# First block's down GEMM two steps late, its last three by token halves, last up step with stationary weights; edges and orders of two sister stages

## The chip, the cores and the metric

The kernel runs on one core of one Trainium2 chip. The metric is the device time of one execution in microseconds (us), taken as the median of several executions. TensorE, VectorE, ScalarE, GpSimd and SyncE are called PE, DVE, ACT, POOL and SP, as in the profile.

## What is computed

Two transformer stacks, one behind the other, on 256 tokens of width 1024, each with two layers, in float32. The part of the reference that the change touches is the feed-forward half of every layer, and the passage from one layer to the next:

```python
# first stack, per layer l
gu = jnp.einsum('bsd,df->bsf', x, w_ffn_in[l])
hidden = jax.nn.silu(gu[..., :D_FF]) * gu[..., D_FF:]
ffn = jnp.einsum('bsf,fd->bsd', hidden, w_ffn_out[l])
x = layer_norm(DN_ALPHA * x + ffn, ln2_g[l], ln2_b[l])
# second stack, per layer i
h = rms_norm_2(x, ffn_norm_g[i]) @ w_up[i]
h = depthwise_conv(h, conv_w[i], conv_b[i])
gate, up = jnp.split(h, 2, axis=-1)
x = x + (jax.nn.silu(gate) * up) @ w_down[i]
```

D_FF is 2816. The attention parts ahead of it (neighbourhood, differential and latent attention in the first stack, grouped attention and spatial gating in the second) are the same computation before and after; one order inside the neighbourhood attention changes.

## The kernel before

**Pieces.** Every weight matrix comes from memory in pieces of at most 128 x 2048 (1 MB). SP loads piece i into one of three buffers `raw`, once DVE has finished with piece i-3. ACT rounds it to `whi` (the matmul's narrower float format; L1098) and DVE subtracts to get the rest, `wlo` (L1585). This is called splitting. There are four slots of `whi`/`wlo`: piece i can be split when PE has used piece i-4. Activations are split in the same way (`xTh`/`xTl`, `aTh`/`aTl`, `bTh`/`bTl`), and every product is the sum of three matmuls, high x high, high x low and low x high.

**Two ways to multiply.** In `gemm` and `half` (L384 to L388, L480 to L482) the activations are the stationary operand, a half of 128 tokens (`th` 0 or 1) at a time, and the weights stream past, 512 columns per matmul. In `by_features` (L409 to L412) the weights are stationary, and the activations of all 256 tokens stream past: one matmul of 512 columns takes high weights with `xTh` and `xTl` at once, one of 256 columns takes low weights with `xTh`. It ends in two PSUM areas that have to be added, ACT copying one out (`low_out`) and DVE adding (`features_out`). Its result has features on the partitions, as the next GEMM wants it; that of `gemm` has tokens there, and has to be transposed on PE.

**The feed-forward of the first stack.** It has NSTEP = 11 steps. Step c has an up GEMM (two pieces, 256 gate and 256 up features) and a down GEMM (one piece). `up(0)` and `up(1)` are by tokens, with a transpose `h_turn` behind; steps 2 to 9 are by features in two pairs of PSUM banks (0,1 and then 2,3); step 10 is by tokens again, in halves that are mixed with the halves of the last two down GEMMs and with two half turns of the hidden block (L813). The down GEMM of step c-1 follows the up GEMM of step c. The hidden blocks alternate in `aTh`/`aTl`.

**Its end, the edge to the next layer.** When token half 0 of the last down GEMM is summed, DVE adds it to x (`add_down`, L1963, one operation), takes the moments (`stats`, L1592 and L1595), POOL raises the variance to the power -0.5 (L289, L291), DVE applies the norm (`apply`, four operations, L1602 and L1604, each pair ending a half of x), PE transposes that half (`turn_x`, L437), ACT rounds it to `xTh` (L1105, or L1117 with gains) and DVE writes `xTl` (L1611, or L1623 with gains). Then the same with token half 1. The next layer's first GEMM needs the transposed x and the next four pieces, here called N0 to N3. Every engine works strictly in the order in which its program was written, so a split stands before or behind these steps by hand.

**The feed-forward of the second stack** is two steps late already: `up(0)` by tokens, then `up_features(c)` for 1 to 10, and `down(c-2)` behind each. `up(0)` ends in banks 0 and 1, from which ACT takes it with a scale (L1533); `by_features` for step 1 begins in bank 0 too. PE transposes step 0 (`conv_turn`, L1027) inside step 1.

**Neighbourhood attention.** For g = 0 to 4 PE computes scores of a pair of heads, transposes probabilities (`turn_probs`, L547) and mixes them with values (`mix_pair`, L557), with parts of other GEMMs between. ACT copies the transposed probabilities out (`probs_out`, L1217); `catch` is the place at which ACT or DVE empties PSUM and splits what may be split, up to `ahead` pieces past those that PE has used.

## Time and profile before

| | |
|---|---|
| median of 3 runs | 1482.4 us (1482.22 to 1482.57) |
| the profiled execution's own time | 1482.46 us |
| its span | 1481.1 us |
| PE, busy share | 98% |
| DVE / ACT / POOL, busy share | 70% / 55% / 4% |
| granted TensorE clock | 0.999 of full speed |
| DMA, mean rate over the span | 176 GB/s |

The span is the time between the first and the last instruction of the profiled execution; 1.4 us of its own time lie around it. A matmul's end is modelled, and a matmul is pipelined with its neighbours, so that the busy share of PE overstates it: two starts in a row lie closer together than one duration. Lines named L... are those of the kernel before.

### The profile page before, as it was taken

Reading aid. Unit: us, or ns where it says so; the run is one execution under the profiler, and the core shown is the slowest. Engines: PE = TensorE matmul, PEld = TensorE weight load, DVE = VectorE, ACT = ScalarE, POOL = GpSimd, SP = SyncE. Lnnn points to the kernel's source line nnn. Section 1 sums busy time; section 2 is a strip of 40 time slices with the busy share of each in tenths; the row PEclk is TensorE's granted clock in tenths of the full one; section 3 lists DMA queues with packets and bytes.
Section 4 is the critical chain, followed back from the end, with each engine's and each line's share of the span. In section 5 each row is a group of like instructions: output and inputs, shape, how many; then the busy total and the mean of one; then the engine's idle time right before and its main releaser. Section 6 shows DMA issues by size and latency. Waiting matters only on the chain.

```text
span 1481.1 us, 19352 instructions
## 1 busy us (share of the span) xinstructions
PE 1451.0 (98%) x7547; PEld 1209.0 (82%) x7547; DVE 1044.1 (70%) x1413; ACT 816.3 (55%) x1163; POOL 65.3 (4%) x100
## 2 busy tenths in 40 slices
PE   6999999999999999999999999899999999999998
PEld 5788887888887787887888888788888888888887
DVE  5656885865556656786775565877888868778886
ACT  3555654444453455654444544586665567766563
POOL 2000000000001000000010000210000012000000
PEclk9999999999999999999999999999999999999999
DMA  8543643566564635543666556336565635356651
GB/s 320 180 153 127 238 170 118 189 228 198 192 206 143 215 118 157 191 138 132 194 230 196 174 186 211 116 114 199 171 198 186 227 127 171 122 175 199 203 184 57
DMA packets 167323, 261.06 MB, mean 176 GB/s; under 512 B 8768, under 2 KB 106720, under 8 KB 166720
## 3 DMA queue, kind: packets, MB, share of 16 engines
q1 hardware_dynamic: 166048, 252.03, 51.8%
q0 software_dynamic: 896, 6.74, 1.2%
q8 instruction: 60, 0.98, 0.3%
q10 hardware_dynamic: 288, 1.05, 0.2%
q14 instruction: 31, 0.25, 0.0%
HBM read 258.74 MB, written 1.05 MB: 175 GB/s over the span
## 4 chain that ended last, share of the span: by engine, by line
PE 83%; DVE 9%; ACT 3%; issue 2%; POOL 1%; DMA 1%; SPq 0%; DVEq 0%; ACTq 0%
PE ps L409 16%; PE ps L480 10%; PE ps L482 10%; PE ps L481 10%; PE ps L410 9%; PE ps L384 7%; PE ps L388 7%; PE ps L386 7%; DVE wlo L1585 3%; PE ps L412 2%; ACT whi L1098 1%; PE ps L534 1%; PE ps L557 1%; DVE x L1604 1%; DVE x L1602 1%
## 5 line engine op out<-in xcount | busy, mean ns | idle before, releaser
L1585 DVE TENSOR_TENSOR wlo<-raw,whi 128x2048 fp32r<-128x2048 f32 (+1 forms) x238 | 528.1, 2229 | 230.3 <-ACT whi L1098 230.3
L1098 ACT ACTIVATE whi<-raw 128x2048 fp32r<-128x2048 f32 (+1 forms) x238 | 441.8, 1866 | 145.0 <-PE ps L482 54.3
L409 PE MATMUL ps<-xT,whi 128*128 128x512 f32 x1008 | 356.4, 395 | 1.6 <-ACT proj L1533 1.6
L410 PE MATMUL ps<-xT,wlo 128*128 128x256 f32 x1152 | 311.1, 280 | 0.0
L480 PE MATMUL ps<-whi,xT 128*128 128x512 f32 (+3 forms) x640 | 251.1, 392 | 8.9 <-DVE xT L1623 3.7
L482 PE MATMUL ps<-whi,xT 128*128 128x512 f32 (+3 forms) x640 | 242.1, 378 | 0.0
L481 PE MATMUL ps<-wlo,xT 128*128 128x512 f32 (+3 forms) x640 | 241.4, 377 | 0.0
L409 PEld LDWEIGHTS ps<-xT,whi 128*128 128x128 f32 x1008 | 189.0, 188 | 44.4 <-ACT proj L1533 2.4
L410 PEld LDWEIGHTS ps<-xT,wlo 128*128 128x128 f32 x1152 | 217.4, 189 | 6.0
L480 PEld LDWEIGHTS ps<-whi,xT 128*128 128x128 f32 x640 | 120.3, 188 | 35.7 <-issue 12.7
L482 PEld LDWEIGHTS ps<-whi,xT 128*128 128x128 f32 x640 | 120.2, 188 | 22.7
L481 PEld LDWEIGHTS ps<-wlo,xT 128*128 128x128 f32 x640 | 120.7, 189 | 18.8
L384 PE MATMUL ps<-whi,aTh 128*128 128x512 f32 x352 | 109.4, 392 | 0.3 <-DVE aTl L2199 0.2
L388 PE MATMUL ps<-whi,aTl 128*128 128x512 f32 x352 | 108.7, 390 | 0.0
L386 PE MATMUL ps<-wlo,aTh 128*128 128x512 f32 x352 | 108.7, 390 | 0.0
L388 PEld LDWEIGHTS ps<-whi,aTl 128*128 128x128 f32 x352 | 66.1, 188 | 14.1
L386 PEld LDWEIGHTS ps<-wlo,aTh 128*128 128x128 f32 x352 | 66.1, 188 | 13.9
L384 PEld LDWEIGHTS ps<-whi,aTh 128*128 128x128 f32 x352 | 65.4, 188 | 14.2 <-DVE aTl L2199 1.1
L2176 DVE SCALAR_TENSOR_TENSOR proj<-proj,rpb 128x255 f32<-128x255 f32 x160 | 70.1, 480 | 9.5 <-ACT proj L1507 8.0
L1381 ACT ACTIVATE prob<-ps 128x512 f32<-128x512 f32 x32 | 19.2, 599 | 70.3 <-PE ps L412 70.3
L1515 ACT ACTIVATE proj<-ps 128x512 f32<-128x512 f32 x40 | 23.5, 588 | 62.1 <-PE ps L412 62.1
L412 PE MATMUL ps<-xT,whi 128*128 128x512 f32 x144 | 53.8, 396 | 0.0
(205 smaller groups left out, 1882.4 us busy)
## 6 DMA issues: line engine op xcount, KB each, us to landing
raw<-in_w_in SPq DMA_DIRECT2D x124, 512.0 KB, 4.7
raw<-in_w_ffn_in SPq DMA_DIRECT2D x88, 512.0 KB, 4.8
raw<-in_w_up SPq DMA_DIRECT2D x88, 512.0 KB, 4.7
raw<-in_w_ffn_out SPq DMA_DIRECT2D x44, 512.0 KB, 4.5
raw<-in_w_down SPq DMA_DIRECT2D x44, 512.0 KB, 4.4
raw<-in_w_branch SPq DMA_DIRECT2D x24, 512.0 KB, 4.8
raw<-in_w_out SPq DMA_DIRECT2D x16, 512.0 KB, 4.4
raw<-in_w_o SPq DMA_DIRECT2D x16, 512.0 KB, 4.5
```

The costliest lines, as they stand in the source:

```text
L384: PE.matmul(o, ah, hi[:, j, b], start=first and kt == 0, stop=False)
L386: PE.matmul(o, ah, lo[:, j, b], start=False, stop=False)
L388: mm = PE.matmul(o, al, hi[:, j, b], start=False, stop=last and j == c - 1 and i == len(kts) - 1)
L409: PE.matmul(ps[:, f, :], hi, m.xT[:, kt], start=kt == 0, stop=False)
L410: mm = PE.matmul(ps[:, f, 0:S], lo, m.xTh[:, kt], start=False, stop=False)
L412: mm = PE.matmul(ps[:, f, :], hi, m.xT[:, kt], start=False, stop=True)
L480: PE.matmul(o, ah, hi[:, j, :], start=kt == 0, stop=False)
L481: PE.matmul(o, ah, lo[:, j, :], start=False, stop=False)
L482: mm = PE.matmul(o, al, hi[:, j, :], start=False, stop=end)
L1098: AC.activation(m.whi[:, i % SPLIT, 0:w], m.raw[:, slot, 0:w], ACT.Copy).then_inc(s.w_hi, 1)
L1585: DV.tensor_tensor(m.wlo[:, i % SPLIT, 0:w], m.raw[:, slot, 0:w], m.whi[:, i % SPLIT, 0:w].bitcast(F32), ALU.subtract).then_inc(s.w_lo, 1)
L2176: a = DV.scalar_tensor_tensor(out=conv[:, f, to], in0=src[:, f, of], scalar=m.cw[:, c, f, tap:tap + 1], in1=conv[:, f, to], op0=ALU.mult, ...
```

## The change

- First stack: the down GEMM of step c-2 follows the up GEMM of step c. Hidden blocks go round three places (`aT` 0-1, `aT` 2-3, `bT` 0-1). Step 10 is by features like 2 to 9. The down GEMMs of steps 8, 9 and 10 run for token half 0 in a row, then for half 1. The two half turns of step 10 are gone; the turns of steps 0 and 1 go to banks 4 and 5, the second in the midst of step 2.
- At its end DVE splits in another order, shown below, and the second `turn_x` of half 0 comes ahead of the last six matmuls, not behind them.
- `by_features` begins with banks 2 and 3, in both stacks; in the second stack PE's wait for ACT's copies of `up(0)` stands at the second pair, `conv_turn` two positions later, and step 10 is computed with three matmuls of 256 columns for each weight block (`joined=False`), into one PSUM area, without `low_out` and without the addition.
- Neighbourhood attention: at g = 3 ACT splits one piece fewer ahead of `probs_out`, and DVE divides the last pair's probabilities already then.

```diff
-def ffn_names(b, L):
-
-    seq = [((b, L, "up", c), (PIECE, PIECE)) for c in range(b)]
-    for c in range(b, NSTEP):
-        seq += [((b, L, "up", c), (PIECE, PIECE)), ((b, L, "dn", c - b), (PIECE,))]
-    return seq + [((b, L, "dn", c), (PIECE,)) for c in range(NSTEP - b, NSTEP)]
+def ffn_names(b, L, lag):
+
+    seq = [((b, L, "up", c), (PIECE, PIECE)) for c in range(lag)]
+    for c in range(lag, NSTEP):
+        seq += [((b, L, "up", c), (PIECE, PIECE)), ((b, L, "dn", c - lag), (PIECE,))]
+    return seq + [((b, L, "dn", c), (PIECE,)) for c in range(NSTEP - lag, NSTEP)]
+
+
+def hidden_blocks(m, c):
+
+    if c % 3 < 2:
+        return [x[:, c % 3 * 2:c % 3 * 2 + 2, :] for x in (m.aTh, m.aTl)]
+    return [x[:, 0:2, :] for x in (m.bTh, m.bTl)]
...
-    def by_features(name, before):
+    def by_features(name, before, first, joined=True):
 
         i0 = k.first[name]
         for pair in range(2):
@@ -403,13 +410,18 @@
                 if pair == 0 and j == 0:
                     PE.wait_ge(s.w_lo, i0 + kt // 4 + 1)
                 for f in (2 * pair, 2 * pair + 1):
-                    o = j * 2 * FC + f * P
+                    o, b = j * 2 * FC + f * P, f ^ first
                     hi, lo = [x[:, slot, o:o + P] for x in (m.whi, m.wlo)]
+                    if not joined:
+                        PE.matmul(ps[:, b, 0:S], hi, m.xTh[:, kt], start=kt == 0, stop=False)
+                        PE.matmul(ps[:, b, 0:S], lo, m.xTh[:, kt], start=False, stop=False)
+                        mm = PE.matmul(ps[:, b, 0:S], hi, m.xTl[:, kt], start=False, stop=end)
+                        continue
                     if not end:
-                        PE.matmul(ps[:, f, :], hi, m.xT[:, kt], start=kt == 0, stop=False)
-                    mm = PE.matmul(ps[:, f, 0:S], lo, m.xTh[:, kt], start=False, stop=False)
+                        PE.matmul(ps[:, b, :], hi, m.xT[:, kt], start=kt == 0, stop=False)
+                    mm = PE.matmul(ps[:, b, 0:S], lo, m.xTh[:, kt], start=False, stop=False)
                     if end:
-                        mm = PE.matmul(ps[:, f, :], hi, m.xT[:, kt], start=False, stop=True)
+                        mm = PE.matmul(ps[:, b, :], hi, m.xT[:, kt], start=False, stop=True)
...
         up(0, before=up_turn)
         PE.wait_ge(s.hidden, n.up("hidden"))
         up(1, (0,))
-        bank_free(2)
-        h_turn()
+        h_turn(4)
         up(1, (1,))
-        h_ready()
-        down(0)
-        h_turn()
-        reads = 2 * (end - 2) * L
-        for c in range(2, end):
+        reads = 2 * (NSTEP - 2) * L
+        for c in range(2, NSTEP):
             def ready(pair, kt):
-                if kt == 0 and c > 2:
+                if c == 2 and not pair:
+                    if kt == 0:
+                        bank_free(2)
+                    if kt == 5:
+                        h_turn(5)
+                elif c > 2 and kt == 0:
                     PE.wait_ge(s.up_read, reads + 2 * (c - 3) + pair + 1)
-                elif kt == 0 and pair:
+
+            by_features((1, L, "up", c), ready, 2)
+            if c < end:
+                h_ready()
+                if c == 2:
                     PE.wait_ge(s.h_lo, n["h_lo"] + 1)
-
-            by_features((1, L, "up", c), ready)
+                down(c - 2)
+        for c in range(NSTEP - 3, NSTEP):
             h_ready()
-            down(c - 1)
-        PE.wait_ge(s.up_read, reads + 2 * (end - 2))
-        up(end, (0,))
-        h_ready()
-        down(end - 1, (0,))
-        up(end, (1,), (0,), before=last_turn)
-        h_ready()
-        down(end, (0,))
-        up(end, (1,), (1,))
-
-        def last_half_turn(th, kt):
-            if kt == 1:
-                h_turn((1,))
-
-        def first_x_turn(th, kt):
-            if kt == 1:
-                turn_x(0, 0)
-
-        down(end - 1, (1,), last_half_turn)
-        h_ready()
-        down(end, (1,), first_x_turn)
-        turn_x(0, 1)
+            down(c, (0,))
+        down(NSTEP - 3, (1,))
+        down(NSTEP - 2, (1,))
+        down(NSTEP - 1, (1,), last_x_turn)
...
-                if kt == 0 and c == 1:
+                if kt == 0 and c == 1 and pair:
                     PE.wait_ge(s.conv_up, 2 * NSTEP * L + 2)
+                elif kt == 0 and c == 1:
                     bank_free(2)
                 elif kt == 0:
-                    PE.wait_ge(s.conv_read, 2 * (NSTEP - 1) * L + 2 * (c - 2) + pair + 1)
-                if c == 1 and pair == 0 and kt in (2, 4):
-                    (conv_turn, root_turn)[kt // 2 - 1]()
-
-            by_features((2, L, "up", c), ready)
+                    PE.wait_ge(s.conv_read, 2 * (NSTEP - 2) * L + 2 * (c - 2) + pair + 1)
+                if c == 1 and pair == 0 and kt in (4, 6):
+                    (conv_turn, root_turn)[kt // 2 - 2]()
+
+            by_features((2, L, "up", c), ready, 2, joined=c < NSTEP - 1)
...
-            catch(1, L, "na", g, 2, ahead=SPLIT - (g == 4))
+            catch(1, L, "na", g, 2, ahead=SPLIT - (g > 2))
...
-            if g:
+            if g in (1, 2, 3):
...
+            if g == 3:
+                normalise_pair(h0, g)
...
-        hidden_half(0)
-        h_lo(slice(0, P))
         split_to(later + 1)
         add_down(0, (1, L, "dn", NSTEP - 1))
-        hidden_half(1)
         for n4 in range(2):
             stats(0, n4)
-        h_lo(slice(P, S))
         DV.wait_ge(s.vec, 32 * (L + 2))
         apply(0)
         if L + 1 < DEPTH:
             turn_lo_quarter(0, 0)
+            split_to(later + 2)
+            turn_lo_quarter(0, 1)
+            split_to(later + 3)
         else:
+            split_to(later + 2)
             DV.wait_ge(s.par, 80)
-            turn_lo_gains(0, 0, 16)
-        split_to(later + 2)
+            for n4 in range(2):
+                turn_lo_gains(0, n4, 16)
...
+            if c == NSTEP - 1:
+                DV.tensor_tensor(feats[:, fs, :], ps[:, 2 - 2 * pair:4 - 2 * pair, 0:S], roots, ALU.mult).then_inc(s.conv_up, 1)
+                return
```

ACT, neighbourhood attention at g = 3 (L1170 copies a GEMM out, `whi<-raw` splits, `probT<-ps` is `probs_out`), before:

```order
L1217 ACTIVATE probT<-ps 128x512 [waits pairs_mixed,probs_turned]
L1170 ACTIVATE gate,small<-ps 128x384 [waits w_used]
L1173 ACTIVATE proj<-ps 128x384
L1098 ACTIVATE whi<-raw 128x2048 [waits w_used,raw2]
L1098 ACTIVATE whi<-raw 128x2048 [waits w_used,raw0]
L1217 ACTIVATE probT<-ps 128x512 [waits pairs_mixed,probs_turned]
L1170 ACTIVATE gate,small<-ps 128x256 [waits th0_sum]
L1173 ACTIVATE proj<-ps 128x288
```

and in the changed kernel:

```order
L1216 ACTIVATE probT<-ps 128x512 [waits pairs_mixed,probs_turned]
L1169 ACTIVATE gate,small<-ps 128x384 [waits w_used]
L1172 ACTIVATE proj<-ps 128x384
L1097 ACTIVATE whi<-raw 128x2048 [waits w_used,raw2]
L1216 ACTIVATE probT<-ps 128x512 [waits pairs_mixed,probs_turned]
L1169 ACTIVATE gate,small<-ps 128x256 [waits th0_sum]
L1172 ACTIVATE proj<-ps 128x288
L1097 ACTIVATE whi<-raw 128x2048 [waits w_used,raw0]
```

The second split moved behind the copy and behind the next GEMM's copy.

DVE, end of the first stack's first layer (`x<-x,ps` is `add_down`, BN rows are `stats`, the four `x<-x` rows are `apply`, `xT<-ps,xT` gives `xTl`, `wlo<-raw,whi` is a split), before:

```order
L1963 SCALAR_TENSOR_TENSOR x<-x,ps 128x1024 [waits th0_sum]
L1976 TENSOR_TENSOR gate<-gate,ps 128x256 [waits up_in,x_sum]
L1592 BN_STATS bn<-x 128x6 x2
L1595 BN_AGGR mv<-bn 128x2 [waits dve_step]
L1980 TENSOR_TENSOR aTl<-ps,aTh 128x2x128 [waits h_hi]
L1602 SCALAR_TENSOR_TENSOR x<-x,mv,vec 128x512 [waits rstd,vec]
L1604 SCALAR_TENSOR_TENSOR x<-x,small,vec 128x512 [waits dve_step]
L1602 SCALAR_TENSOR_TENSOR x<-x,mv,vec 128x512
L1604 SCALAR_TENSOR_TENSOR x<-x,small,vec 128x512 [waits dve_step]
L1611 SCALAR_TENSOR_TENSOR xT<-ps,xT 128x4x128 [waits turn_hi]
L1585 TENSOR_TENSOR wlo<-raw,whi 128x2048 [waits w_hi]
L1963 SCALAR_TENSOR_TENSOR x<-x,ps 128x1024 [waits w_used]
```

and in the changed kernel, from `apply` of half 0 on:

```order
L1598 SCALAR_TENSOR_TENSOR x<-x,mv,vec 128x512
L1600 SCALAR_TENSOR_TENSOR x<-x,small,vec 128x512 [waits dve_step]
L1607 SCALAR_TENSOR_TENSOR xT<-ps,xT 128x4x128 [waits turn_hi]
L1581 TENSOR_TENSOR wlo<-raw,whi 128x2048 [waits w_hi]
L1607 SCALAR_TENSOR_TENSOR xT<-ps,xT 128x4x128 [waits turn_hi]
L1581 TENSOR_TENSOR wlo<-raw,whi 128x2048 [waits w_hi]
L1961 SCALAR_TENSOR_TENSOR x<-x,ps 128x1024 [waits w_used]
```

The two operations on the half block (L1976, L1980) are gone; between `apply` of half 0 and `add_down` of half 1 there are now two splits and two quarters of `xTl`, before one split and one quarter. Between `stats` and `apply` of half 1 there is one split, before there were two in this layer and one in the second. In the second layer the first split there (N1) stands ahead of both `xTl` quarters, and only one split (N1) lies before `add_down` of half 1.

PE, second stack, where step 1 by features begins (`ps<-ident,proj` is `conv_turn`), before:

```order
L409 MATMUL ps<-xT,whi 128x512 [waits w_lo,free2,conv_up]
L410 MATMUL ps<-xT,wlo 128x256
...
L409 MATMUL ps<-xT,whi 128x512
L410 MATMUL ps<-xT,wlo 128x256
L1027 MATMUL ps<-ident,proj 128x128 [waits conv_up]
```

and in the changed kernel the same place:

```order
L421 MATMUL ps<-xT,whi 128x512 [waits w_lo,free2]
L422 MATMUL ps<-xT,wlo 128x256
...
L421 MATMUL ps<-xT,whi 128x512
L422 MATMUL ps<-xT,wlo 128x256
L1025 MATMUL ps<-ident,proj 128x128 [waits conv_up]
L1025 MATMUL ps<-ident,proj 128x128 x7
L421 MATMUL ps<-xT,whi 128x512 [waits w_lo]
```

The wait `conv_up` left the first matmul. It now stands at the transposes, which begin 16 matmuls behind the first instead of 8.

## Rows read from the trace of the kernel before

**Rows 1.** The page's first line.
```profile
span 1481.1 us, 19352 instructions
```

**Rows 2.** PE's waits: who for whom: us in total, times, longest.
```profile
PE ps L480 <- DVE xT L1623: 3.7, 4, 1.5
...
PE ps L557 <- ACT probT L1217: 2.5, 3, 1.1
...
PE ps L409 <- ACT proj L1533: 1.6, 2, 0.8
```

**Rows 3.** PE's timeline (start, us, engine, line, op, tiles, count): three passages, first and next.
```profile
332.21 0.39 PE L409 MATMUL ps<-xT,whi 128*128 128x512 f32 x1
...
343.41 0.62 PE L384 MATMUL ps<-whi,aTh 128*128 128x512 f32 x2
...
448.83 0.39 PE L384 MATMUL ps<-whi,xT 128*128 128x512 f32 x1
...
454.27 0.62 PE L384 MATMUL ps<-whi,aTh 128*128 128x512 f32 x2
...
949.73 0.28 PE L480 MATMUL ps<-whi,xT 128*128 128x256 f32 x1
...
952.61 0.40 PE L480 MATMUL ps<-whi,xT 128*128 128x512 f32 x1
```

**Rows 4.** Groups by line and shape, weight loads of L409.
```profile
L409 PEld LDWEIGHTS ps<-xT,whi 128*128 128x128 f32 x1008 | 189.0, 188 | 44.4 <-ACT proj L1533 2.4
```

**Rows 5.** Timelines of PE and ACT, neighbourhood attention at g = 3.
```profile
99.40 0.87 PE L557 MATMUL ps<-probT,proj 128*64 128x256 f32 x6 [1.12 <-ACT probT L1217]
...
95.14 3.71 ACT L1098 ACTIVATE whi<-raw 128x2048 fp32r<-128x2048 f32 x2
```

**Rows 6.** PE's timeline, the second half turn of step 10.
```profile
923.69 0.38 PE L813 MATMUL ps<-ident,gate 128*128 128x128 f32 x2
923.82 0.71 PE L384 MATMUL ps<-whi,aTh 128*128 128x512 f32 x2
```

**Rows 7.** PE's timeline, first matmul behind half 0 of the last down, both layers.
```profile
462.69 0.39 PE L384 MATMUL ps<-whi,xT 128*128 128x512 f32 x1
...
919.60 0.39 PE L384 MATMUL ps<-whi,xT 128*128 128x512 f32 x1
```

**Rows 8.** DVE's timeline at the edges behind the first stack's layers 0 and 1.
```profile
475.96 0.69 DVE L1611 SCALAR_TENSOR_TENSOR xT<-ps,xT 128x512 fp32r<-128x512 f32 x1
...
482.88 0.75 DVE L1602 SCALAR_TENSOR_TENSOR x<-x,mv,vec 128x512 f32<-128x512 f32 x1 [0.44 <-POOL small L291]
...
921.30 1.21 DVE L1963 SCALAR_TENSOR_TENSOR x<-x,ps 128x1024 f32<-128x1024 f32 x1
...
923.34 1.28 DVE L1592 BATCH_NORM_STATS2 bn<-x 128x6 f32<-128x512 f32 x2
...
925.91 0.75 DVE L1602 SCALAR_TENSOR_TENSOR x<-x,mv,vec 128x512 f32<-128x512 f32 x1 [0.47 <-POOL small L291]
926.70 0.75 DVE L1604 SCALAR_TENSOR_TENSOR x<-x,small,vec 128x512 f32<-128x512 f32 x1
...
929.50 1.13 DVE L1623 SCALAR_TENSOR_TENSOR xT<-ps,pcol,xT 128x128 fp32r<-128x128 f32 x4 [0.60 <-ACT xT L1117]
...
936.34 0.21 DVE L1595 BATCH_NORM_AGGREGATE mv<-bn 128x2 f32<-128x12 f32 x1
936.47 2.24 DVE L1585 TENSOR_TENSOR wlo<-raw,whi 128x2048 fp32r<-128x2048 f32 x1
939.43 0.75 DVE L1602 SCALAR_TENSOR_TENSOR x<-x,mv,vec 128x512 f32<-128x512 f32 x1 [0.72 <-POOL small L291]
```

**Rows 9.** POOL's timeline at the second edge, halves 0 and 1.
```profile
924.96 0.19 POOL L289 TENSOR_SCALAR small<-mv 128x1 f32<-128x1 f32 x1 [174.71 <-DVE mv L1595]
...
936.64 2.12 POOL L289 TENSOR_SCALAR small<-mv 128x1 f32<-128x1 f32 x1 [2.46 <-DVE mv L1595]
```

**Rows 10.** PE's timeline, second stack, first matmul of the last down.
```profile
1199.36 0.73 PE L384 MATMUL ps<-whi,aTh 128*128 128x512 f32 x2 [0.22 <-DVE aTl L2199]
```

More of the change, by code:

```diff
@@ L806, in tensor_program, with h_turn @@
             mark((1, L, "w", 3 + i))
-        def h_turn(ths=(0, 1)):
-            b = ps[:, 2, :].rearrange("p (k s) -> p k s", k=2)
+        def h_turn(bank):
+            b = ps[:, bank, :].rearrange("p (k s) -> p k s", k=2)
             PE.wait_ge(s.hidden, n.up("hidden"))
             for kt in range(2):
-                for th in ths:
+                for th in range(2):
                     mm = PE.transpose(b[:, kt, th * P:(th + 1) * P], gate_cols(kt, th), m.ident[:])
@@ L821, in down @@
         def down(c, ths=(0, 1), before=None):
-            gemm((1, L, "dn", c), (2,), narrow, 512, aT, first=c == 0, last=c == NSTEP - 1, toff=c % 2 * 2,
-                 ths=ths, before=before)
+            gemm((1, L, "dn", c), (2,), narrow, 512, hidden_blocks(m, c), first=c == 0, last=c == NSTEP - 1, ths=ths,
+                 before=before)
         def up_turn(th, kt):
@@ L835, in h_ready, with last_x_turn @@
             PE.wait_ge(s.h_lo, n.up("h_lo"))
-        def last_turn(th, kt):
-            if kt == 2:
-                h_turn((0,))
+        def last_x_turn(th, kt):
+            turn_x(0, kt)
         up(0, before=up_turn)
@@ L1377, in scalar_program @@
         split()
-        h_hi()
+        h_hi(0)
         def low_out(c, pair):
             wait_sum((1, L, "up", c), pair)
-            AC.activation(m.prob[:, 2 + pair], ps[:, 2 * pair:2 * pair + 2, S:2 * S], ACT.Copy).then_inc(s.up_low, 1)
+            AC.activation(m.prob[:, 2 + pair], ps[:, 2 - 2 * pair:4 - 2 * pair, S:2 * S], ACT.Copy).then_inc(s.up_low, 1)
         def gate_silu():
@@ L1388, in features_hi @@
             AC.wait_ge(s.up_out, n.up("up_out"))
-            AC.wait_ge(s.w_used, k.after[1, L, "dn", c - 2])
-            AC.activation(m.aTh[:, c % 2 * 2:c % 2 * 2 + 2, :], m.prob[:, 1], ACT.Copy).then_inc(s.h_hi, 1)
+            if c > 2:
+                AC.wait_ge(s.w_used, k.after[1, L, "dn", c - 3])
+            AC.activation(hidden_blocks(m, c)[0], m.prob[:, 1], ACT.Copy).then_inc(s.h_hi, 1)
         split()
         up_in(1)
-        split()
-        h_hi(b=2)
-        split()
-        for c in range(2, NSTEP - 1):
+        h_hi(1)
+        for c in range(2, NSTEP):
+            up = (1, L, "up", c)
             low_out(c, 0)
             gate_silu()
-            split()
+            split_to(k.after[up] - 1 + SPLIT)
             low_out(c, 1)
-            split()
+            if c < NSTEP - 1:
+                split_to(k.after[up] + SPLIT)
             features_hi(c)
-            split()
+            if c < NSTEP - 1:
+                split_to(k.after[1, L, "dn", c - 2] + SPLIT)
         later = k.after[1, L, "dn", NSTEP - 1]
-        up_in_half(NSTEP - 1, 0)
-        h_hi(slice(0, P))
-        split_to(later + 1)
-        up_in_half(NSTEP - 1, 1)
         split_to(later + 2)
-        h_hi(slice(P, S))
         if L + 1 < DEPTH:
@@ L1542, in scalar_program @@
             up = (2, L, "up", c)
-            low_out(c, 0)
+            if c < NSTEP - 1:
+                low_out(c, 0)
             hidden_hi(c - 1)
-            if c == NSTEP - 1:
-                low_out(c, 1)
-            else:
+            if c < NSTEP - 1:
                 split_to(k.after[up] - 1 + SPLIT)
@@ L1995, in features_out @@
                 DV.wait_ge(s.h_lo, n["h_hi"])
-            DV.tensor_tensor(m.prob[:, pair], ps[:, 2 * pair:2 * pair + 2, 0:S], m.prob[:, 2 + pair], ALU.add).then_inc(s.up_read, 1)
+            DV.tensor_tensor(m.prob[:, pair], ps[:, 2 - 2 * pair:4 - 2 * pair, 0:S], m.prob[:, 2 + pair], ALU.add).then_inc(s.up_read, 1)
         def features_gated():
```

51 lines of the change are left out of this document (24 added, 27 removed).

## The prediction

> **What bounds the kernel now.** I read the page first [rows 1], then the list of PE's waits [rows 2], then the timelines of PE, DVE, ACT and POOL around each wait that the change touches. PE is almost never idle: the waits of [rows 2] are a few microseconds in a span of 1481.1. So PE's own sequence is the bound, and a change can win only PE time that is spent on nothing, or PE work. Two facts of PE are needed for every step. A step by features takes 343.41 - 332.21 = 11.20 us; half a step by tokens, 24 matmuls of 512 columns, takes 454.27 - 448.83 = 5.44, that is 0.227 per matmul [rows 3]. Each such matmul is drawn 0.39 long, 0.16 more than the distance to the next, so a wait that vanishes gives back its printed idle time plus up to 0.16.
>
> **Attention at g = 3.** PE stands 1.12 us before it mixes, waiting for ACT's copy; ACT was busy with two splits in a row, 95.14 to 98.85 [rows 5]. The change puts one of them behind the copy. A split is half of 3.71, so the copy ends near 97.6 instead of 99.4, before PE arrives. The moved split is done some 2.2 later than before, but the GEMM that needs that piece is still more than a microsecond away by the order of work (a full half of 24 matmuls of 288 columns stands between), and DVE's division of the last pair now comes before DVE has to wait for that split. Gain 1.2 per layer; both layers of the first stack have it (the wait is listed three times, 2.5 in total, [rows 2]). Term: **-2.4**.
>
> **Start of the second stack's feed-forward.** PE waits 0.8, twice, for ACT's copy of `up(0)` (L1533) out of banks 0 and 1 [rows 2]. Step 1 now begins in banks 2 and 3, which nobody reads. The wait moves to the transposes, 16 matmuls or 2.8 us further on, when the copy is long over. What is late next is `conv_turn` and the chain behind it, by about 0.3 us in absolute time; step 2 asks for its result a whole step later, so this is hidden. Gain 2 x (0.78 + 0.16). Term: **-1.9**.
>
> **Last step of the second stack, unjoined.** 96 matmuls of 256 columns take the place of 32 pairs of 512 and 256. The trace has such a stream: 24 matmuls of 256 columns, each with its own load of 128 x 128, take 952.61 - 949.73 = 2.88, that is 0.120 each [rows 3]. 96 x 0.120 = 11.52, against 11.20: +0.3 per layer. In return ACT's two copies and DVE's two additions go, and the chain to the last hidden block is shorter by about 2 us. PE's wait for that block, 0.22 in the first layer [rows 10], goes (0.38 with the 0.16), the second layer has none in the list. Term: 0.6 - 0.4 = **+0.2**. Bounds of the disputed price: by columns alone 96 x 0.113 = 10.9, and if no load overlapped with the next one 96 x 0.188 = 18.0 [rows 4]. I take 0.120, since its row is the same operation with the roles of the operands swapped.
>
> Here a rule speaks against the change. The Trainium skill, TensorE: Matmul & The Clock Gate, The mechanism, says that weight loads overlap with running matmuls only when their row group differs, and LDWEIGHTS (loading the stationary operand) gives 128 / 1.2 = 107 ns for a load. By that rule a matmul of 256 columns would cost 107 + 113 = 220 ns, the step 21 us, and the kernel 19 us more than by my term. The spacing of 0.120 above disagrees with it: these loads use all rows and overlap all the same.
>
> **First stack, the order of the steps.** Two steps late instead of one changes no instruction count, and nothing waited on this path before. Hidden blocks in three places keep a block alive until its down GEMM is through. Step 10 by features costs 11.20 instead of 2 x 5.44 = 10.88, +0.3; one half turn less ahead of the edge gives back 0.13 plus the 0.09 by which the next two matmuls are stretched [rows 6]. The last block's hidden values are ready about 3.9 us after the step (ACT copy, DVE add and product, ACT and DVE rounding, each 0.6 to 0.7, with no split between them any more), and PE has two halves of a down GEMM, 5.44, in front of that use: hidden, with 1.5 to spare. Term: 2 x 0.1 = **+0.2**.
>
> **First stack, the two edges.** This is the largest term. Let T be the start of the first matmul behind half 0 of the last down GEMM: 462.69 and 919.60 before [rows 7]. In both programs the same PE work lies between T and the next layer's second token half (three half downs or their equivalent, two `turn_x`, two half GEMMs of the next layer), apart from the other half turn. What ends last is DVE's chain: the transposes of half 1 wait for `apply` of half 1, which begins at 482.88 and 939.43 [rows 8], that is T + 20.2 and T + 19.8. From there on the sequences are equal. So I walk DVE's new order from T with the durations of [rows 8].
>
> Half 0: the sum is there 0.2 after T; `add_down` 1.25 (before, it had to wait for a split and began at T + 1.7 in the second layer). From the first `stats` to `apply` 925.91 - 923.34 = 2.6, to the end of `apply` 3.0 more (four operations of 0.75). The first half of x is normed at 0.2 + 1.25 + 2.6 + 1.5 = T + 5.6, where PE arrives at T + 5.44: a wait of 0.2. `apply` ends at T + 7.0.
>
> Second layer: split N1 2.2 (T + 9.2), two quarters with gains of 1.13, the second held a little by ACT (T + 11.6), `add_down` of half 1 1.25, `stats` 1.3 (T + 14.2), then to `apply` 939.43 - 936.34 = 3.1. It begins at T + 17.3, against 19.8: **-2.5**. First layer: quarter 0.7, N1 2.2, quarter 0.7, N2 2.2 (T + 12.8), `add_down` 1.25, `stats` 1.3, 3.1: T + 18.4, against 20.2: -1.8. There the 3.1 holds because only one split now lies behind `stats`: under a split POOL's first operation takes 2.12 instead of 0.19 [rows 9]; before, two splits covered both of POOL's operations there. In the first layer PE could itself be there at T + 19.7 when the norm is through at T + 19.9, so no more can be had. Term: -2.5 - 1.8 = **-4.3**. It holds if the loads of N1 to N3 are landed; they are issued as in the kernel before, as soon as DVE frees the buffer.
>
> **Sum.** -2.4 - 1.9 + 0.2 + 0.2 - 4.3 = -8.2. The profiled execution took 1482.46 of its own (span 1481.1, 1.4 around it), 0.06 above the median of 1482.4, so both bases give 1474.2.
>
> **Rivals.**
> 1. *The edges keep their length.* Every link in them is an in-order step on DVE, and one late event (a load of N2 or N3, ACT's rounding behind a split) pushes all that follows. In the second layer N1 is now split ahead of the quarters that PE waits for first, which costs PE about 1 us there that it doesn't wait now; I count it as absorbed by the later chain. Against it: the walk has DVE as the only late engine. Time: 1474.2 + 4.3 = 1478.5.
> 2. *The unjoined steps are bound by weight loads.* For it: a load is drawn 0.188 long, longer than a matmul of 256 columns needs. Against it: 0.120 in [rows 3]. Price: 192 x (0.188 - 0.120) = 13.1 in both layers, 1487.3, slower than before. It decides from a spacing of 0.120 + (8.2 + 3.0) / 192 = 0.178 on. By the skill's rule above the time would be 1474 + 19 = 1493.
> 3. *The last hidden block is late.* In the kernel before, splits stood in the chain from the last step by features to its hidden block and stretched it; if one still falls there (2.2), the block comes at 6.1 instead of 3.9 and PE waits 0.7 per layer: 1475.6, inside the forecast's range.
> 4. *Nothing moves*: waits taken away come back at the next event of the same engine. Attention and the start of the second stack would have to give back all they win. 1482.
>
> **How the numbers follow.** The forecast, 1472.5 to 1477, has 0.72, with rival 3 in it. Rival 1 has 0.16 (1477 to 1479.4). Rival 4 0.06. Rival 2 0.04, of which the skill's rule is 0.01. 0.02 lies below 1472. A measurement of this kernel tells 0.2%, 3.0 us, from no change: faster is below 1479.4, same up to 1485.4. That makes 0.90, 0.06, 0.04. The range reaches from 1471.8 to 1479.2.
>
> **What the profile would show.** If right: no wait at the mixing of g = 3; the first matmul of step 1 in the second stack without idle time, and none at its transposes; a step of about 11.5 for the unjoined one; from T to `apply` of half 1 17.3 and 18.4 us; small waits of 0.2 to 1.1 at the four `turn_x` of each edge, and about 1 us in the second layer ahead of the next layer's first matmul. The prediction is wrong if `apply` of half 1 begins no earlier than 19.8 after T, if a split or a load shows as the releaser of PE's waits in the edges, or if the spacing of the unjoined matmuls is near 0.19.

## The result, and the profile after

The changed kernel takes **1472.34 us** (median of 4 runs, 1472.25 to 1472.51) against 1482.38 (1482.22 to 1482.57) for the kernel before: 10.0 us less, ratio 0.9932 with a 95% interval of 0.9919 to 0.9946. Forecast were 1474.2 and 1471.8 to 1479.2. The time lies inside the range, but below 1472.5, where the band that had 0.72 of the chances begins. The profiled execution has a span of 1471.1 us, against [rows 1], at a granted clock of 1.0.

The list of PE's waits after (who for whom: us in total, times, longest), to be held against [rows 2]:

```profile
PE ps L449 <- DVE x L1600: 2.4, 7, 0.8
PE ps L492 <- DVE xT L1619: 2.3, 3, 1.1
PE ps L492 <- DVE wlo L1581: 0.9, 2, 0.6
PE ps L492 <- DVE xT L1607: 0.8, 1, 0.8
...
PE ps L569 <- ACT probT L1216: 0.3, 1, 0.3
```

One line of the same view of the kernel before is needed beside it:

```profile
PE ps L480 <- DVE xT L1611: 3.1, 2, 2.1
```

The wait for ACT's copy of `up(0)` is gone, and so is the one for the last hidden block. The mixing (now L569) waits 0.3 where it waited 2.5. The quarters of `xT` with gains cost 2.3 where they cost 3.7. Those without gains fell from 3.1 to 0.8, but this is not all gain of the change: the 2.1 of before and the 0.8 of after are the same wait at 16 us, at the start of the program, which swings between profiles (0.8 in that of `banks_alone`, which starts like the kernel before). Only the other one, 0.98 at 476.79, belongs to an edge.

At each of the following places PE has done the same share of the computation in both kernels, so the difference of two starts is what has been gained up to there, less what the changed steps cost PE (starts in the timelines of before and after, us):

| first matmul of | before | after | difference |
|---|---|---|---|
| the first GEMM's later matmuls | 41.94 | 41.35 | -0.6 |
| mixing at g = 3, layer 0 | 99.40 | 97.59 | -1.8 |
| work behind half 0 of the last down (T), layer 0 | 462.69 | 460.94 | -1.75 |
| a mixing in layer 1 | 528.72 | 524.71 | -4.0 |
| mixing at g = 3, layer 1 | 556.12 | 550.93 | -5.2 |
| T, layer 1 | 919.60 | 914.42 | -5.2 |
| 256-column part of the second stack's first GEMM | 938.81 | 930.88 | -7.9 |
| step 1, second stack, layer 0 | 1031.25 | 1022.36 | -8.9 |
| the GEMM behind step 10, layer 0 | 1188.07 | 1179.49 | -8.6 |
| last down, layer 0 | 1199.36 | 1190.40 | -9.0 |
| the next layer's first GEMM | 1209.93 | 1200.81 | -9.1 |
| step 1, layer 1 | 1303.50 | 1293.43 | -10.1 |
| the GEMM behind step 10, layer 1 | 1460.32 | 1450.56 | -9.8 |
| last down, layer 1 | 1471.40 | 1461.46 | -9.9 |
| near the end of it | 1476.07 | 1466.00 | -10.1 |

Two edges (-2.3 and -2.7), two places in attention (-1.2 each) and two starts of a feed-forward (-1.0 each) are nearly all of it; 0.6 is there already in the first row.

ACT's and PE's timelines after, at g = 3 (start, us, engine, line, op), where [rows 5] stood:

```profile
94.53 1.92 ACT L1097 ACTIVATE whi<-raw 128x2048 fp32r<-128x2048 f32 x1
96.34 0.60 ACT L1216 ACTIVATE probT<-ps 128x512 f32<-128x512 f32 x1
...
97.97 1.91 ACT L1097 ACTIVATE whi<-raw 128x2048 fp32r<-128x2048 f32 x1
```

```profile
97.59 0.87 PE L569 MATMUL ps<-probT,proj 128*64 128x256 f32 x6
```

The copy ends at 96.94, before PE has finished the matmuls ahead of the mixing, and PE's row has no idle time in brackets.

PE's timeline after, first matmul of step 1 in the second stack, and the unjoined step (first, second and the GEMM behind):

```profile
1022.36 0.39 PE L421 MATMUL ps<-xT,whi 128*128 128x512 f32 x1
...
1167.98 0.28 PE L416 MATMUL ps<-xT,whi 128*128 128x256 f32 x1
1168.09 0.28 PE L417 MATMUL ps<-xT,wlo 128*128 128x256 f32 x1
...
1179.49 0.63 PE L391 MATMUL ps<-whi,aTh 128*128 128x512 f32 x2
```

No wait at the first; the step takes 1179.49 - 1167.98 = 11.51.

DVE's timeline after, at the second edge, T = 914.42 (compare [rows 8]):

```profile
911.87 2.29 DVE L1581 TENSOR_TENSOR wlo<-raw,whi 128x2048 fp32r<-128x2048 f32 x1 [1.11 <-ACT whi L1097]
914.62 1.22 DVE L1961 SCALAR_TENSOR_TENSOR x<-x,ps 128x1024 f32<-128x1024 f32 x1 [0.47 <-PE ps L395]
...
918.45 0.75 DVE L1598 SCALAR_TENSOR_TENSOR x<-x,mv,vec 128x512 f32<-128x512 f32 x1 [1.04 <-POOL small L298]
...
921.35 2.28 DVE L1581 TENSOR_TENSOR wlo<-raw,whi 128x2048 fp32r<-128x2048 f32 x1
923.55 2.38 DVE L1619 SCALAR_TENSOR_TENSOR xT<-ps,pcol,xT 128x128 fp32r<-128x128 f32 x8
...
928.42 0.21 DVE L1591 BATCH_NORM_AGGREGATE mv<-bn 128x2 f32<-128x12 f32 x1
928.54 2.24 DVE L1581 TENSOR_TENSOR wlo<-raw,whi 128x2048 fp32r<-128x2048 f32 x1
931.50 0.75 DVE L1598 SCALAR_TENSOR_TENSOR x<-x,mv,vec 128x512 f32<-128x512 f32 x1 [0.72 <-POOL small L298]
```

The norm of half 1 begins at T + 17.08, before at T + 19.83; in layer 0 it begins at 479.13 = T + 18.19, before T + 20.19. Most of this is won ahead of the norm of half 0: that begins at T + 4.03, before at 925.91 - 919.60 = T + 6.31. The addition of half 0 started at 921.30 = T + 1.7 before, since a split was in its way; after, that split is over before T. Layer 0 shows the same (addition and norm of half 0, before with T = 462.69, after with T = 460.94):

```profile
464.38 1.21 DVE L1963 SCALAR_TENSOR_TENSOR x<-x,ps 128x1024 f32<-128x1024 f32 x1
...
468.98 0.75 DVE L1602 SCALAR_TENSOR_TENSOR x<-x,mv,vec 128x512 f32<-128x512 f32 x1 [0.46 <-POOL small L291]
```

```profile
461.14 1.22 DVE L1961 SCALAR_TENSOR_TENSOR x<-x,ps 128x1024 f32<-128x1024 f32 x1 [0.19 <-PE ps L395]
...
464.95 0.75 DVE L1598 SCALAR_TENSOR_TENSOR x<-x,mv,vec 128x512 f32<-128x512 f32 x1 [1.03 <-POOL small L298]
...
479.13 0.75 DVE L1598 SCALAR_TENSOR_TENSOR x<-x,mv,vec 128x512 f32<-128x512 f32 x1 [0.72 <-POOL small L298]
```

PE's waits in this edge, from its timeline after:

```profile
924.82 0.47 PE L492 MATMUL ps<-whi,xT 128*128 128x512 f32 x1 [0.90 <-DVE xT L1619]
...
933.10 0.66 PE L449 MATMUL ps<-ident,x 128*128 128x128 f32 x4 [0.19 <-DVE x L1600]
...
934.54 0.65 PE L449 MATMUL ps<-ident,x 128*128 128x128 f32 x4 [0.43 <-DVE x L1600]
...
936.24 0.47 PE L492 MATMUL ps<-whi,xT 128*128 128x512 f32 x1 [0.33 <-DVE xT L1619]
```

One more wait, 0.36 at 930.88, has no releaser in the view. It ends 0.10 behind the end of the split between the moments and the norm of half 1 (928.54 + 2.24 = 930.78), as that of 0.58 at 938.81 did before (936.47 + 2.24 = 938.71). So PE probably waits for that split's piece there, and it comes earlier only because DVE's whole chain does.

The last hidden block of the first stack is a place where PE doesn't wait, but only just. DVE's timeline after, in layer 0, and PE's first use:

```profile
452.46 2.29 DVE L1581 TENSOR_TENSOR wlo<-raw,whi 128x2048 fp32r<-128x2048 f32 x1 [3.67 <-ACT whi L1097]
454.67 0.68 DVE L1995 TENSOR_TENSOR prob<-ps,prob 128x512 f32<-128x512 f32 x1
...
456.85 0.69 DVE L2005 TENSOR_TENSOR aTl<-prob,aTh 128x512 fp32r<-128x512 f32 x1 [0.70 <-ACT aTh L1391]
```

```profile
458.22 0.61 PE L391 MATMUL ps<-whi,aTh 128*128 128x512 f32 x2
```

### The profile page after: what moved, and what is told of

It is laid out like the page before. It is cut to its first block, busy times and chain, and to the rows that moved or that the text cites. A ratio compares the mean times of both kernels' runs of the same rounds, so it can differ in the third digit from the quotient of the medians.

```text
span 1471.1 us, 19474 instructions
## 1 busy us (share of the span) xinstructions
PE 1449.6 (99%) x7635; PEld 1215.1 (83%) x7635; DVE 1043.9 (71%) x1409; ACT 815.8 (55%) x1159; POOL 62.4 (4%) x100
## 3 DMA queue, kind: packets, MB, share of 16 engines
q10 hardware_dynamic: 288, 1.05, 0.2%
HBM read 258.74 MB, written 1.05 MB: 177 GB/s over the span
## 4 chain that ended last, share of the span: by engine, by line
PE 85%; DVE 9%; ACT 3%; issue 1%; POOL 1%; DMA 1%; SPq 0%; DVEq 0%; ACTq 0%
PE ps L421 16%; PE ps L492 10%; PE ps L494 10%; PE ps L493 10%; PE ps L422 9%; PE ps L391 6%; PE ps L395 6%; PE ps L393 6%; DVE wlo L1581 3%; PE ps L424 2%; PE ps L546 1%; PE ps L559 1%; PE ps L569 1%; PE ps L449 1%; DVE x L1600 1%
## 5 line engine op out<-in xcount | busy, mean ns | idle before, releaser
L391 PE MATMUL ps<-whi,aTh 128*128 128x512 f32 x304 | 94.1, 391 | 0.0
L393 PE MATMUL ps<-wlo,aTh 128*128 128x512 f32 x304 | 93.9, 390 | 0.0
L395 PE MATMUL ps<-whi,aTl 128*128 128x512 f32 x304 | 93.9, 390 | 0.0
L395 PEld LDWEIGHTS ps<-whi,aTl 128*128 128x128 f32 x304 | 57.0, 188 | 12.3
L393 PEld LDWEIGHTS ps<-wlo,aTh 128*128 128x128 f32 x304 | 57.1, 188 | 12.0
L391 PEld LDWEIGHTS ps<-whi,aTh 128*128 128x128 f32 x304 | 56.5, 188 | 10.5
L1504 ACT ACTIVATE proj<-proj,rpb 128x256 f32<-128x256 f32 x80 | 43.5, 591 | 13.7 <-DVE proj L2188 11.4
```

What stands on the lines that cost most here:

```text
L391: PE.matmul(o, ah, hi[:, j, b], start=first and kt == 0, stop=False)
L393: PE.matmul(o, ah, lo[:, j, b], start=False, stop=False)
L395: mm = PE.matmul(o, al, hi[:, j, b], start=False, stop=last and j == c - 1 and i == len(kts) - 1)
```

## The experiments

Each kernel ran beside the kernel before, which took 1481.9 to 1482.3 there. "Up to a place" means, as in the table above, PE's start there against the changed kernel's profile. From one profile to the next the first place of that table already differs by up to 0.73 us (41.35 to 42.08), in kernels that change nothing there; the figures below are taken from steps in the difference, and medians are given beside them.

### The changed kernel once more

> The changed kernel itself, on the same chip as the three kernels that follow, as their anchor. Its start differed from that of the kernel before by 0.4 to 0.6 us up to the first GEMM, and so did that of other kernels which change nothing there. Theory: that is chance, so that its span varies by some tenths, and the median stays at 1472.3 to 1472.8.

Measured: 1472.42 (before: 1482.18). Its profile is 0.37 late at the start and stays 0.3 to 0.45 late to the end. The 0.6 of the table's first row can be chance of this kind, and medians of two such kernels a few tenths apart tell little by themselves. Whether all of it is chance stays open: the two profiles that start like the kernel before have that place at 41.94 and 41.96, those of the changed kernel and of its variants at 41.34 to 42.08, with 41.6 in the middle.

### Attention undone

```diff
-            catch(1, L, "na", g, 2, ahead=SPLIT - (g > 2))
+            catch(1, L, "na", g, 2, ahead=SPLIT - (g == 4))
...
-            if g in (1, 2, 3):
+            if g:
                 normalise_pair(h0, g - 1)
...
-            if g == 3:
-                normalise_pair(h0, g)
```

> The changed kernel with the neighbourhood attention's edit undone (two splits ahead of ACT's second copy at g = 3, DVE's division at g = 4). My theory: a wait of PE at the mixing of g = 3 costs its idle time plus 0.16 in each layer and nothing downstream absorbs it, so this kernel takes 2.3 us longer than the changed one, 1474.6. Rival (waits only move to the next event of the engine): within 0.5 us of the changed kernel, 1472.3 to 1472.8.

Measured: 1474.93, 2.6 above the changed kernel's first median (2.3 were expected). The steps in the difference are +1.29 and +1.13, at the mixing of g = 3 in each layer, and nowhere else. Nothing downstream gives them back.

### The order of banks alone, in the kernel before

```diff
-                if kt == 0 and c == 1:
+                if kt == 0 and c == 1 and pair:
                     PE.wait_ge(s.conv_up, 2 * NSTEP * L + 2)
+                elif kt == 0 and c == 1:
                     bank_free(2)
...
-            by_features((2, L, "up", c), ready)
+            by_features((2, L, "up", c), ready, 2)
```

> The kernel before, with only the order of banks, the place of the wait and of the two turns of the second stack's feed-forward taken from the change. Theory: PE's wait for ACT's copy of step 0 goes in both layers and no other part of the change is needed for it: 1.7 to 1.9 us under the kernel before, 1480.6. Rival: the gain needs the earlier end of the first stack or the unjoined last step; then under 0.5 us, 1482.

Measured: 1480.25 against 1482.25. Against the profile of before there is a step of -1.05 at step 1 in layer 0 and -0.99 in layer 1. The gain is there without the rest of the change.

### The last step of the second stack joined again

```diff
-            by_features((2, L, "up", c), ready, 2, joined=c < NSTEP - 1)
+            by_features((2, L, "up", c), ready, 2)
...
-            if c == NSTEP - 1:
-                DV.tensor_tensor(feats[:, fs, :], ps[:, 2 - 2 * pair:4 - 2 * pair, 0:S], roots, ALU.mult).then_inc(s.conv_up, 1)
-                return
```

> The changed kernel with the last step of the second stack joined again (512 and 256 columns, ACT's copies and DVE's additions back). Theory: 0.3 us less matmul time in each layer, against a wait of 0.38 for the last hidden block in the first: the time moves by less than 0.3 us either way, 1472.2 to 1472.6. Rival A: the unjoined step is worth its shorter chain, 0.5 to 1 us slower when it is joined. Rival B: the 256-column matmuls cost more than they look, 1471.5 or less when it is joined.

Measured: 1472.96, 0.6 above the first median; of this 0.35 lies ahead of the edit in the profile. Behind it: -0.32 in each layer for the shorter step, then +0.50 in layer 0 and +0.30 in layer 1, where the last down waits for its hidden block (PE's idle time there is printed as 0.22 and 0.02 only). The unjoined step is worth 0.2 us in all; that PE pays 0.3 more than the printed time was not expected.

### Thirty-four more steps unjoined

```diff
+                    if name[0] == 2 or name[3] > 2:
+                        PE.matmul(ps[:, b, 0:S], hi, m.xTh[:, kt], start=kt == 0, stop=False)
+                        PE.matmul(ps[:, b, 0:S], lo, m.xTh[:, kt], start=False, stop=False)
+                        mm = PE.matmul(ps[:, b, S:2 * S], hi, m.xTl[:, kt], start=False, stop=end)
+                        continue
```

> The changed kernel with 34 more steps by features (second stack 1 to 9, first stack 3 to 10, both layers) as three matmuls of 256 columns per weight block, in the same two PSUM areas, so that all else stays. Theory: 0.120 us per matmul also when steps follow each other, 11.52 per step against 11.20: 34 x 0.32 = 10.9 us more, 1483.3. If loads bound it, at 0.188 each, a step takes 18.0 and the kernel about 230 us more; if loads did not overlap at all, 0.22 each, over 330 us more. If the other engines' waits are absorbed by the longer steps, a little less than 10.9.

Measured: 1483.33, 11.0 above the changed kernel. Each of the 34 steps adds 0.32. PE's timeline of this kernel, the end of a step:

```profile
345.81 0.28 PE L421 MATMUL ps<-xT,whi 128*128 128x256 f32 x1
345.93 0.28 PE L422 MATMUL ps<-xT,wlo 128*128 128x256 f32 x1
346.05 0.28 PE L423 MATMUL ps<-xT,whi 128*128 128x256 f32 x1
```

The distance is 0.12, each with a load of its own of 128 x 128. Rival 2 of the prediction is out.

### DVE's order of before, at both edges

```diff
         if L + 1 < DEPTH:
             turn_lo_quarter(0, 0)
-            split_to(later + 2)
-            turn_lo_quarter(0, 1)
-            split_to(later + 3)
         else:
-            split_to(later + 2)
             DV.wait_ge(s.par, 80)
-            for n4 in range(2):
-                turn_lo_gains(0, n4, 16)
+            turn_lo_gains(0, 0, 16)
+        split_to(later + 2)
         add_down(1, (1, L, "dn", NSTEP - 1))
+        if L + 1 < DEPTH:
+            turn_lo_quarter(0, 1)
+        else:
+            turn_lo_gains(0, 1, 16)
```

> The changed kernel with DVE's order at both edges as in the kernel before (one quarter, split N1, addition of half 1, the other quarter, its moments, then the rest of the splits), without the half hidden block that stood there before. Theory A (what shortened the edges is that the half block's operations left DVE's chain; the order alone is worth little): half 1's norm begins at T + 18.2 and T + 17.1 as in the changed kernel, PE waits 0.7 for the late quarter instead, and the kernel is 0 to 0.4 us slower than the changed one. Theory B (the new order made it): 1.5 to 3 us slower, half 1's norm at T + 19 or later.

Measured: 1472.83 against 1472.42 of the changed kernel in the same comparison. Steps in the difference: +0.05 at the first edge, +0.43 at the second. DVE's timeline of this kernel at the first edge, T = 460.94:

```profile
470.68 1.21 DVE L1961 SCALAR_TENSOR_TENSOR x<-x,ps 128x1024 f32<-128x1024 f32 x1
471.93 0.69 DVE L1607 SCALAR_TENSOR_TENSOR xT<-ps,xT 128x512 fp32r<-128x512 f32 x1
...
473.97 4.44 DVE L1581 TENSOR_TENSOR wlo<-raw,whi 128x2048 fp32r<-128x2048 f32 x2
478.85 0.75 DVE L1598 SCALAR_TENSOR_TENSOR x<-x,mv,vec 128x512 f32<-128x512 f32 x1 [0.44 <-POOL small L298]
```

The norm of half 1 comes at T + 17.9, even earlier than in the changed kernel (18.19); what is late is a quarter that PE needs, and PE makes that up before the edge ends. At the second edge the norm comes at 931.98, T + 17.5, which is 0.5 later than the 17.1 that theory A had for it, because DVE stands 0.60 for ACT's `xTh` there. The size is theory A's, and theory B's 1.5 to 3 is out: of the 5.0 us that the edges gained, the order of what follows the norm of half 0 made 0.5.

### The first quarter ahead of the split, second edge

```diff
         else:
-            split_to(later + 2)
             DV.wait_ge(s.par, 80)
-            for n4 in range(2):
-                turn_lo_gains(0, n4, 16)
+            turn_lo_gains(0, 0, 16)
+            split_to(later + 2)
+            turn_lo_gains(0, 1, 16)
```

> The changed kernel with split N1 between the two quarters with gains at the second edge, not ahead of both. Theory: the wait of 0.90 ahead of the next layer's first matmul goes, but the norm of half 1 still begins at T + 17.1 and bounds the edge, so that PE waits longer at the transposes of half 1 and the time stays within 0.2 us of the changed kernel. Rival (PE's own waits count there): 0.9 us faster.

Measured: 1472.80 against 1472.42. PE starts the next GEMM 0.79 earlier (924.03 against 924.82, in a profile that is 0.27 late up to there) and then loses 1.96 where it lost 0.52 (at 931.64, 0.10 behind the end of the next split): the step over the whole edge is +0.48. The rival failed, as the theory had it, but the theory, which had at most 0.2, missed a loss: a quarter taken first makes DVE stand for ACT's `xTh` (0.60 in the same place of the kernel just above), and the split used that time.

### A later addition

```diff
         split_to(later + 1)
+        DV.wait_ge(s.th0_sum, k.call[1, L, "dn", NSTEP - 1])
+        g = m.gate[:, 0, 0:D]
+        then(DV.tensor_tensor(g, g, m.vec[:, 0:D], ALU.mult))
         add_down(0, (1, L, "dn", NSTEP - 1))
```

> The changed kernel with one operation more on DVE (128 x 1024, two inputs in SBUF, a scratch result that nobody uses), after half 0 of the last down GEMM is summed and ahead of the addition, in both layers of the first stack; it puts the addition back by about 1.2 us, where the kernel before had it (T + 1.7) or a little ahead. Theory (both edges are bound by DVE's chain from the sum of half 0 to the norm of half 1): each edge gets longer by the whole 1.2, 2.4 us over the changed kernel, 1474.8. Rival (there is slack in the edges, PE would have been late anyway): under 1 us in all.

Measured: 1474.98. The operation takes 1.26 from start to start, and the steps are +1.25 and +1.26, each at the first transpose of half 0, and nothing of them is given back up to the end of the edge. Both edges are bound by DVE's chain, one for one: what is won ahead of the norm of half 0 is won in full.

### The last split ahead of the moments

```diff
+        split_to(later + 3 + (L + 1 < DEPTH))
         for n4 in range(2):
             stats(1, n4)
-        split_to(later + 3 + (L + 1 < DEPTH))
         apply(1)
```

> The changed kernel with the last split of each edge ahead of the moments of half 1, not between them and the norm, so that POOL's two operations have no split beside them. Theory: POOL's first operation takes 0.19 and not 2.12, the norm comes 1.24 after the moments instead of 2.95, the split's own 2.2 stands ahead of it: the norm of half 1 0.5 us later in each layer, 0.6 to 1.0 us slower than the changed kernel. Rival (POOL's 2.12 is its own, whatever DVE does): it stays at 2.12 and the kernel is over 4 us slower.

Measured: 1472.87; steps of +0.27 and +0.25, half of the 0.5 that the theory had for each layer. POOL's timelines at the second edge, first of the changed kernel (under the split), then of this one:

```profile
928.72 2.12 POOL L296 TENSOR_SCALAR small<-mv 128x1 f32<-128x1 f32 x1 [2.00 <-DVE mv L1591]
930.91 0.55 POOL L298 TENSOR_TENSOR small<-small,half 128x1 f32<-128x1 f32 x1
```

```profile
931.48 0.19 POOL L296 TENSOR_SCALAR small<-mv 128x1 f32<-128x1 f32 x1 [4.20 <-DVE mv L1591]
931.75 0.55 POOL L298 TENSOR_TENSOR small<-small,half 128x1 f32<-128x1 f32 x1
```

The same operation takes 0.19 without a split beside it; the rival is out. The split still belongs where it was: ahead of the moments it costs its own 2.2 (the norm then comes 932.34 - 931.18 = 1.16 behind them), between them and the norm only 3.08 - 1.16 = 1.9. The difference of 0.3 is the step measured.

### One split earlier in the second stack

```diff
+        if L + 1 < DEPTH:
+            split_to(k.after[2, L, "dn", NSTEP - 2] + SPLIT - 1)
         for th in range(2):
...
             if not th and L + 1 < DEPTH:
                 DV.wait_ge(s.par, 32 + 48 * (L + 2))
-                split_to(k.after[2, L, "dn", NSTEP - 2] + SPLIT - 1)
```

> The changed kernel with one split of DVE moved at the end of the second stack's first layer: from between the addition of half 0 and xTl to ahead of the addition, where DVE stands idle for 3 us. Theory: xTl then waits for ACT's xTh alone and begins at 1196.3 instead of 1196.72 of the span, PE's wait of 1.08 there becomes 0.65: 0.4 us faster than the changed kernel. Rival: the split delays the addition and with it the chain: same or slower.

Measured: 1472.01 against 1472.42; a step of -0.3 at 1197.99, the first matmul of the next layer, and none elsewhere. The expected step was 0.4. By its trace this kernel is a little faster than both, by an amount that the medians alone would not tell.

### One operation of POOL moved to DVE

```diff
-        PO.tensor_scalar(dst, m.mv[:, th, 1:2], 1.0, LN_EPS, ALU.mult, ALU.add).then_inc(s.pool_step, 1)
-        PO.wait_ge(s.pool_step, n.up("step"))
-        PO.tensor_tensor(dst, dst, m.half[:, 0:1], ALU.pow).then_inc(s.rstd, 1)
+        PO.tensor_tensor(dst, m.mv[:, th, 1:2], m.half[:, 0:1], ALU.pow).then_inc(s.rstd, 1)
...
-            DV.bn_aggr(m.mv[:, th, :], m.bn[:, th, :, :].rearrange("p a b -> p (a b)")).then_inc(s.moments, 1)
+            then(DV.bn_aggr(m.mv[:, th, :], m.bn[:, th, :, :].rearrange("p a b -> p (a b)")))
+            DV.tensor_scalar(m.mv[:, th, 1:2], m.mv[:, th, 1:2], 1.0, LN_EPS, ALU.mult, ALU.add).then_inc(s.moments, 1)
```

> A version meant to beat both: the changed kernel with the early split of the second stack (0.4 us) and, in every layer norm, DVE adding the epsilon to the variance (128 x 1) so that POOL has one operation and not two between the moments and the norm. Theory: at the edges POOL's 0.55 behind the split goes, against 0.15 to 0.2 for DVE's small operation: the norm of half 1 comes 0.4 us earlier in each layer, that of half 0 at the same time; 0.4 + 0.8 = 1.2 us under the changed kernel, 1471.2. Rival (the small operation and its step on DVE cost as much as POOL's): only the 0.4 of the early split, 1472.0.

Measured: 1471.86, the lowest median of all, but only 0.15 under the one just above, and the executions of the two overlap (1471.69 to 1472.08, 1471.95 to 1472.71). The 1471.2 of the theory was not reached. DVE's timeline of this kernel, second edge, from the moments of half 1, and POOL's:

```profile
927.94 0.21 DVE L1589 BATCH_NORM_AGGREGATE mv<-bn 128x2 f32<-128x12 f32 x1
928.19 0.15 DVE L1590 TENSOR_SCALAR mv<-mv 128x1 f32<-128x1 f32 x1
928.26 2.28 DVE L1579 TENSOR_TENSOR wlo<-raw,whi 128x2048 fp32r<-128x2048 f32 x1
930.98 0.75 DVE L1597 SCALAR_TENSOR_TENSOR x<-x,mv,vec 128x512 f32<-128x512 f32 x1 [0.45 <-POOL small L296]
```

```profile
928.42 2.53 POOL L296 TENSOR_TENSOR small<-mv,half 128x1 f32<-128x1 f32 x1 [2.17 <-DVE mv L1590]
```

From the moments to the norm it takes 3.04, in the changed kernel 931.50 - 928.42 = 3.08. The small operation puts the split back by 0.2, and the power still needs 0.44 behind the split. The rival was right at the covered half; at the uncovered half 0 a tenth was won (in the second layer the norm of half 0 begins at T + 3.93, in the changed kernel at T + 4.03).

## Why the prediction was right

The direction, the places and most of the mechanisms were right, and the time came out 1.9 us under the forecast. It is inside the range, but not in the band of 1472.5 to 1477 that was given 0.72: 1472.34 lies in a stretch, 1472.0 to 1472.5, that got no chance of its own. The terms that were off are off to the same side, so they did not help each other out.

**Attention**: forecast -2.4, measured -1.2 twice, and 2.4 when undone alone. The idle time plus 0.16 was the right price of a wait here.

**Start of the second stack**: forecast -1.9, measured -1.0 twice, and 2.0 alone in the other kernel. The later transposes did not wait.

**Unjoined step**: the price, 11.52 forecast, 11.51 measured, 0.32 more per step in 34 further steps. The term was +0.2, and it came out as -0.2, in the table (+0.3 and -0.5 in layer 0, +0.3 and -0.3 in layer 1) and in the joined kernel alike. What failed is the price of the wait behind the step. In layer 0, 0.22 of idle time was worth 0.5 and not 0.38, and in layer 1, where the forecast had no wait, 0.3 was lost at a printed 0.02. Why these cost more than the waits in attention no run shows. The 34 steps became 11 us longer. The Trainium skill's rule on weight loads (TensorE: Matmul & The Clock Gate, The mechanism), which spoke against the change, would by an estimate from that page's 107 ns for a load have made them over 300 us longer; these rows disagree with it. The same section also lets a load go ahead when it targets the background weight buffer; no run here can show which buffer a load used.

**Order of the first stack's steps**: forecast +0.1 per layer, measured 0.05 and 0.0 up to T. The last hidden block (rival 3) wasn't waited for, but the forecast had its chain wrong: it said that no split stands in it any more, and one does. DVE's split from 452.46 holds the addition back to 454.67, while ACT's copy had ended at 452.95 + 0.60 = 453.55. The block is ready at 456.85 + 0.69 = 457.54, 4.8 us after the step (its last matmuls make way at 452.76) and not 3.9, 0.7 before its first use at 458.22 and not 1.5. In layer 1 it is 4.5 and 1.0. So rival 3's event took place, at half its price, and there was room for it.

**Edges**: forecast -4.3, measured -5.0 (-2.26 and -2.75). This is the term that was mis-sized. From T to the norm of half 1 I had 18.4 and 17.3, measured are 18.19 and 17.08: durations rounded up to tenths nine times over, where DVE's operations start 0.05 to 0.1 before the one ahead has ended. The rest, 0.26, is in layer 0 behind the norm: there PE itself came late at the transposes before (485.23, when the first half of x had been normed at 483.67 + 0.75 = 484.42), which I had said can't be had. Of the small waits foreseen at the four `turn_x` of each edge there is one in the first (0.79) and two in the second (0.19 and 0.43).

What my walk did not set apart is where these 5.0 come from. It laid old and new order side by side, and the reader could take the new order of splits for the cause. Two things ahead of it made nearly all: the split that stood in front of the addition until T + 1.7 is over before T (1.5 per layer), and the half hidden block's operations with their waits for ACT left the way (0.8: from the addition to the norm of half 0 it took 925.91 - 921.30 = 4.61, now 918.45 - 914.62 = 3.83). The 1.5 and the 0.8 are read from the two timelines; no run puts the half block back alone. The later addition shows that this part counts in full; DVE's order of before, put back, costs only 0.5.

**Sum**: -8.2, with -0.7 more from the edges, -0.1 from step 10 and -0.4 from the unjoined step, is -9.4. With the 0.6 at the start of the program this makes the 10.0 between the spans of the two profiles. But the start moves by as much between profiles of kernels with the same start, and by medians the change is worth 10.0 in one comparison and 9.8 in the other. So 0.4 to 0.6 us of the gain has no shown cause; the change touches nothing ahead of the table's first place.

**Rival 1** (edges keep their length) fell, and rival 4 with it: the 0.9 us wait that it named is there at 924.82, as forecast, and was absorbed by the later chain; removing it gained nothing.

## What to carry to other kernels

When PE is busy 98% of the time, add up its few waits by place, and for each ask whose chain ends last; in this kernel the gains at separate places added up. In a chain of in-order steps, first look for what stands ahead of its first operation: here that made nearly all, and the order further down the chain 0.5 of 5.0. Removing a wait that a later one of the same chain absorbs gained nothing here, so find the last one before reordering for the first.

## What the runs showed of the hardware

- A POOL operation on one column that starts just behind a DVE split (two inputs in SBUF, 2.24) takes 2.12, alone 0.19, and ends 0.06 after the split; a power alone takes 0.55, behind a split 2.53, and ends 0.4 after it. So it does not get done before the DVE operation has ended. The Trainium skill, SBUF — State Buffer, SBUF: two separate sides, says that a DVE operation with two SBUF inputs and a GpSimd operation that reads SBUF lock each other out, and that whichever starts first holds the shared ports for its whole instruction; these rows agree.
- One more operation of 128 x 1 on DVE between two dependent ones put the split behind it back by 0.2 (it starts 0.32 behind the moments, not 0.12), more than its 0.15. From the moments to the norm this left 3.04 of 3.08.
- A wait of PE can cost more than its printed idle time: 1.12 printed was worth 1.1 to 1.3, 0.78 was worth 1.0, 0.22 was worth 0.5.
- In the profile of the last kernel ACT waited 1.68 for a weight load, up to 999.55, where the changed kernel's profile has the same split at 998.72 without such a wait; PE lost 0.45 by it. Whether that is chance or the loads' limit for a faster kernel stays open.
